# Transformed token blocks for the feed-forward products, built from PSUM and rounded earlier, with four additions fewer

## The reference, cut to what matters

```python
def conv_ffn(u, w_up, conv_w, conv_b, w_down):     # u: 512 x 1024, w_up: 1024 x 5632
    h = u @ w_up
    h = lax.conv_general_dilated(h, conv_w[:, None, :], window_strides=(1,),
                                 padding=((CONV_W - 1, 0),),
                                 dimension_numbers=('NWC', 'WIO', 'NWC'),
                                 feature_group_count=2 * D_FF) + conv_b
    gate, up = jnp.split(h, 2, axis=-1)
    return (jax.nn.gelu(gate, approximate=True) * up) @ w_down

# in reference():
        u = rmsnorm(h, g_pre_ffn[i])
        h = h + rmsnorm(conv_ffn(u, w_ffn_up[i], conv_w[i], conv_b[i], w_ffn_down[i]), g_post_ffn[i])
```

## Time and profile before

| | us |
|---|---|
| median of three runs | 853.69 |
| lowest and highest of them | 853.60, 855.11 |
| the profiled execution | 852.13 |
| its span, first to last instruction | 850.3 |
| TensorE busy | 835.8 (98%) |
| DVE busy | 652.0 (77%) |
| ACT busy | 477.4 (56%) |
| POOL busy | 399.8 (47%) |

### The profile page before, as it was taken

The page is one execution under the profiler, slowest core; times in us unless marked ns, Lnnn a source line. Parts: engine busy times, 40 slices in busy tenths (PEclk is TensorE's granted clock), DMA queues, the critical chain, the costliest instruction groups (busy, mean ns, idle before and its releaser), DMA issues.

```text
span 850.3 us, 13362 instructions
## 1 busy us (share of the span) xinstructions
PE 835.8 (98%) x4685; PEld 729.3 (86%) x4685; DVE 652.0 (77%) x1251; ACT 477.4 (56%) x898; POOL 399.8 (47%) x512
## 2 busy tenths in 40 slices
PE   8999999999999999999999999989999999999997
PEld 7888888888888888999998898879999999888885
DVE  6677787788766668965543589988888887799895
ACT  6566666877666654534452437365555554455562
POOL 5454434243333446986776427665555556100002
PEclk9999999999999999999999999999999999999999
DMA  7541233322223222343337432455544333745494
GB/s 218 164 126 51 71 80 95 94 78 80 82 81 81 63 62 65 110 137 100 88 123 255 142 125 85 157 167 167 167 120 118 118 118 119 278 162 195 151 290 156
DMA packets 138790, 109.24 MB, mean 128 GB/s; under 512 B 7559, under 2 KB 122191, under 8 KB 137700
## 3 DMA queue, kind: packets, MB, share of 16 engines
q1 hardware_dynamic: 137242, 101.00, 39.2%
q0 software_dynamic: 576, 4.19, 1.3%
q10 hardware_dynamic: 906, 3.20, 1.0%
HBM read 96.00 MB, written 12.37 MB: 127 GB/s over the span
## 4 chain that ended last, share of the span: by engine, by line
PE 87%; DVE 7%; DMA 2%; ACT 1%; POOL 1%; issue 1%; SPq 0%; DVEq 0%; ACTq 0%
PE banks L2234 22%; PE banks L2236 22%; PE banks L2235 22%; PE banks L2509 3%; PE banks L2511 3%; PE banks L2510 3%; PE banks L2410 2%; PE banks L2319 2%; PE banks L2318 2%; DVE wide L2060 2%; PE banks L2682 1%; PE banks L2681 1%; PE banks L2680 1%; PE banks L2382 1%; DMA ring_raw<-in_w_ffn_up_dram 1%; DVE pages L2001 1%
## 5 line engine op out<-in xcount | busy, mean ns | idle before, releaser
L845 POOL TENSOR_TENSOR ring_lo<-ring_raw,ring_hi 128x256 fp32r<-128x256 f32 x380 | 312.4, 854 | 271.5 <-ACT ring_hi L1001 271.2
L2234 PE MATMUL banks<-u_hi,ring_hi 128*128 128x512 f32 (+1 forms) x624 | 237.1, 380 | 2.5 <-DVE wide L2060 1.8
L2236 PE MATMUL banks<-u_hi,ring_lo 128*128 128x512 f32 (+1 forms) x624 | 232.2, 372 | 0.0
L2235 PE MATMUL banks<-u_lo,ring_hi 128*128 128x512 f32 (+1 forms) x624 | 232.0, 372 | 0.0
L2234 PEld LDWEIGHTS banks<-u_hi,ring_hi 128*128 128x128 f32 x624 | 118.1, 189 | 21.7 <-DVE wide L2060 2.0
L2236 PEld LDWEIGHTS banks<-u_hi,ring_lo 128*128 128x128 f32 x624 | 118.0, 189 | 20.9
L2235 PEld LDWEIGHTS banks<-u_lo,ring_hi 128*128 128x128 f32 x624 | 118.1, 189 | 18.6
L1001 ACT CAST ring_hi<-ring_raw 128x1024 fp32r<-128x1024 f32 x96 | 100.0, 1043 | 37.7 <-PE banks L2236 24.3
L2060 DVE SCALAR_TENSOR_TENSOR wide<-banks,cols,wide 128x511 f32<-128x511 f32 x88 | 64.8, 746 | 18.9 <-ACT wide L1361 11.4
L852 POOL TENSOR_SCALAR norm_ms<-norm_ss 128x1 f32<-128x1 f32 x15 | 6.0, 401 | 137.4 <-ACT pages L1011 137.3
L2234 PE MATMUL banks<-pages,ring_hi 128*128 128x512 f32 (+1 forms) x176 | 60.1, 341 | 0.0
(11 more groups left out here) (318 smaller groups left out, 1954.6 us busy)
## 6 DMA issues: line engine op xcount, KB each, us to landing
ring_raw<-in_w_ffn_up_dram SPq DMA_DIRECT2D x88, 256.0 KB, 3.4
ring_raw<-in_w_in_dram SPq DMA_DIRECT2D x60, 256.0 KB, 3.4
ring_raw<-in_w_ffn_down_dram SPq DMA_DIRECT2D x55, 256.0 KB, 3.4
ring_raw<-in_w_gate_dram SPq DMA_DIRECT2D x48, 256.0 KB, 3.2
ring_raw<-in_w_out_dram SPq DMA_DIRECT2D x16, 256.0 KB, 3.1
split_tokens<-pages SPq DMA_DIRECT2D x4, 1024.0 KB, 6.8
pages<-split_tokens POOLq DMA_DIRECT2D x4, 1024.0 KB, 11.9
second_tokens<-wide SPq DMA_DIRECT2D x10, 384.0 KB, 4.1
```

The costliest lines, as they stand in the source:

```text
L845: last = pool.tensor_tensor(wlo[:, r, c], raw[:, r, c], whi[:, r, c].bitcast(F32), ALU.subtract)
L2234: pe.matmul(out, lhs_hi, rhs_hi, start=start, stop=False)
L2235: pe.matmul(out, lhs_hi, rhs_lo, start=False, stop=False)
L2236: return pe.matmul(out, lhs_lo, rhs_hi, start=False, stop=stop)
```

## The change

`t_forms_12` makes T1 and T2 with the second token half read straight from banks 4 to 7 (`turned_half`) instead of from the sum of its high and low parts. So the additions of U12 and U22 fall away, two for each part, four in all. `t_forms_34` makes T3 and T4, with T3 now taken from T2 and U11 (T2 - U11). The order is changed on three engines. On DVE, T1 and T2 of part 1 come before the first taps, T3 and T4 of part 1 in their old place, and the low parts of all forms move from pair 1 into pair 0. On ACT, the forms are rounded one by one as each is made, ahead of the taps of unit 0 and of unit 1; in pair 1 the rounding of the weight forms of pair 2 moves ahead of `split_tokens(1)`. On TensorE, the wait for the low parts of the forms moves ahead of the first of the seven products. No matmul, no transfer and no instruction of POOL or SP is added or removed.

```diff
+        T_RAW = {1: 1, 2: 3, 3: 0, 4: 2}
+
+        def turned_half(row, c):
+
+            banks = psum[:, 4:8, :].rearrange("p (t h) (k n) -> p h k t n", h=2, n=P)
+            return banks[:, row, 2 * c:2 * c + 2, :, :]
...
-            def t_forms_high(c):
-
-                act.wait_ge(t_form_sums, 6 * c + 10)
-                for q in range(1, 5):
-                    act.copy(t_form(q, slice(2 * c, 2 * c + 2))[0], u_raw(U_RAW[q], c)).then_inc(t_form_hi, 1)
-
-            for j in range(2):
-                ffn_unit(j, None, j)
-                t_forms_high(j)
+            def t_forms_high(c, which=(1, 2, 3, 4)):
+
+                for q in which:
+                    act.wait_ge(t_form_sums, 4 + 4 * c + q)
+                    act.copy(t_form(q, slice(2 * c, 2 * c + 2))[0], u_raw(T_RAW[q], c)).then_inc(t_form_hi, 1)
+
+            t_forms_high(0)
+            ffn_unit(0, None, 0)
+            t_forms_high(1)
+            ffn_unit(1, None, 1)
...
             gelu(1, 1)
+            up_forms_high(2)
             split_tokens(1)
-            up_forms_high(2)
...
-            def t_sums_rest(c):
...
+            def t_forms_12(c):
+
+                t1, t2, r11 = (u_raw(q, c).rearrange("p k (t n) -> p k t n", n=P) for q in (1, 3, 0))
+                dve.tensor_tensor(t1, turned_half(0, c), r11, sub).then_inc(t_form_sums, 1)
+                dve.wait_ge(t_form_sums, 5 + 4 * c)
+                dve.tensor_tensor(t2, turned_half(1, c), t1, sub).then_inc(t_form_sums, 1)
+
+            def t_forms_34(c):
+
+                r11, r21, t2 = (u_raw(q, c) for q in (0, 2, 3))
+                dve.wait_ge(t_form_sums, 6 + 4 * c)
+                dve.tensor_tensor(r11, t2, r11, sub).then_inc(t_form_sums, 1)
+                dve.tensor_tensor(r21, r21, t2, sub).then_inc(t_form_sums, 1)
...
-            dve.wait_ge(u_lo_done, 2 * TT)
-            t_sums_rest(0)
+            dve.wait_ge(t_form_sums, 4)
+            t_forms_12(0)
+            t_forms_34(0)
+            t_forms_12(1)
...
             ffn_taps(0, None, 0, (0,))
-            t_sums_rest(1)
+            t_forms_34(1)
             ffn_taps(0, None, 0, (1,))
+            t_forms_low(0)
             ffn_product(0, 0, first_tokens)
             ffn_taps(1, None, 1)
+            t_forms_low(1)
             ffn_product(1, 1, second_raw[:, 0:512])
             token_sums(0)
...
                 ffn_taps(2 * i, i, 0, (0,))
-                if i == 1:
-                    t_forms_low(0)
-                else:
+                if i in SEVEN_UP:
                     up_forms_low(i)
                 ffn_taps(2 * i, i, 0, (1,))
                 ffn_product(2 * i, 0, first_tokens)
-                if i == 1:
-                    t_forms_low(1)
...
                 n = i - SEVEN_UP[0]
+                if n == 0:
+                    pe.wait_ge(t_form_lo, 8)
```

More of the change, by code:

```diff
@@ L2000, in t_forms_low @@
                     hi, lo = t_form(q, slice(2 * c, 2 * c + 2))
-                    dve.tensor_tensor(lo, u_raw(U_RAW[q], c), hi.bitcast(F32), sub).then_inc(t_form_lo, 1)
+                    dve.tensor_tensor(lo, u_raw(T_RAW[q], c), hi.bitcast(F32), sub).then_inc(t_form_lo, 1)
             def up_weight_sums(i):
@@ L2629, in seven_up @@
                 n = i - SEVEN_UP[0]
+                if n == 0:
+                    pe.wait_ge(t_form_lo, 8)
                 pe.wait_ge(w_lo_done, up_tile(i, 0) + 1)
                 one_of_seven(W_BANK, up_quarter(0, 0), quarter(0, 0)).then_inc(up_prod, 1)
-                if n == 0:
-                    pe.wait_ge(t_form_lo, 8)
-                else:
+                if n >= 1:
                     pe.wait_ge(up_edge, 2 * n)
```

## The result

The changed kernel takes 845.24 us (four executions, 845.11 to 845.29), the kernel before 853.64 in the same measurement (853.38 to 855.11): a ratio of 0.9898, with a 95% interval of 0.9881 to 0.9915. That is 8.4 us less.

A forecast was written before the change was run, and what follows sets the result against it. TensorE, busy 98% of the span, was taken as the bound, recoverable only at two waits for DVE and a slow-clock stretch. DVE's terms summed to -5.21 us at L2033, giving 848.5 us from the 853.69 median, range 846.6 to 850.9.

The forecast's parts named there:

- the first stop and its half clock: TensorE's 1.79 us idle before unit 2 near 521 and the 1.2 GHz stretch after it (1.73 us): both would go.
- the swap on ScalarE: `up_forms_high(2)` ahead of `split_tokens(1)`: removes DVE's idle before the first taps of unit 4, -1.97 us.
- I predict the median: Final step: 5.2 us off the profiled 852.13 gives 846.9; from the 853.69 median it predicts 848.5 us.
- the second stop: TensorE's 3.11 us wait for `up_edge` (L2033) before pair 2's last product, ending at 569.38; forecast to shrink to 1.4 us.
- rival 3: The clock falls behind the remaining stop, costing 1.73 us: saves 3.5, 850.2 us; chance 0.11.
- my cap of 6.6 us: Most that could be gained on TensorE: 1.79 idle, 1.73 slow clock and 3.11 idle, 6.63 us in all.
- two sums for six behind the first taps: DVE after unit 0's first tap pair makes two sums of half 1 instead of six: -4.31 us.
- The last row keeps its distance: DVE's order from the taps at 556.06 to L2033 is unchanged, so L2033 moves 5.2 us, from 568.81 to 563.6.
- Rival 1: ScalarE's idle is not used, so DVE's 1.97 us before 556.06 stay: saves 3.2, 850.5 us; chance 0.14.
- Rival 2: TensorE's second wait goes wholly, by 1.4 us more from DVE: saves 6.6, 847.1 us; chance 0.11.
- rival 4: The slow stretch at 523.8 has another cause and stays, losing only 0.3 us: 848.8 us; chance 0.10.
- Rivals 5 and 6: No change, L2033 held by something unmoved, 853.7 us (0.05 and 0.03 chances); or slower, late weight tile 8 starving TensorE.

The follow-up runs named there:

- b_again: The kernel before, unchanged, run and profiled again: median 853.91 us of twelve executions, the profiled one 852.46 us.
- b_fill1: The kernel before with 14 idle-time matmuls into an unused bank ahead of TensorE's first long wait: 853.59 us, ratio 1.0.
- b_fill2: The kernel before with 24 idle-time matmuls at TensorE's second long wait alone: 852.34 us, ratio 0.9985.

## Why the prediction was wrong

The mechanism held: the first stop and its half clock went, L2033's place on DVE decided, the wait that was left stood where I had put it (though with 0.47 us for a forecast of 1.4, and so not the longest), the swap on ScalarE took out 1.97 us to the hundredth, and the new idle in unit 2 was 1.37 us (forecast 1.41). None of the new waits of the rivals came. Wrong was the size, by 3.3 us, in two steps.

**First, the baseline (about 1.5 us).** The failed step is "I predict the median": I took the gain from one execution and subtracted it from the median of others, as if both had lost the same. The median stood 1.56 us above the profiled time, and I gave no reason for that. The runs show the reason: half clock behind the second stop, absent in the one profile and present in two of the four later ones in which that stop was not filled (b_again and b_fill1 have none), where it cost 2.55 and 1.57 us; with that stop filled (b_fill2) the median falls by 1.4 us. In rival 3 I took "3.11 us at the second place was not [followed by it]" as evidence that such a stop leaves the clock alone. It was one draw. The gain had one more term, some 1.4 us of clock behind the second stop, and my cap of 6.6 us left it out. What else parts the executions of before, which differ by up to 3 us at the same mean clock, stays open.

**Second, the sum for L2033 (5.2 forecast, 6.81 measured).** Up to the taps of unit 4 DVE moved by 556.06 - 550.23 = 5.83 us; the rest, 0.98 us, is from there to L2033. By my own terms, each measured from the start of its first instruction to the start of the next thing, in us:

| term | forecast | measured |
|---|---|---|
| two sums for six behind the first taps | -4.31 | -4.60 |
| the start, and the sums before those taps | 0 | -0.18 |
| `t_forms_low(0)` | 0 | +0.38 |
| `t_forms_low(1)` | +0.61 | +1.34 |
| products of units 0, 1, 2, 3 | 0 | -1.04 |
| token sums of pair 0 | -0.95 | -0.97 |
| weight sums of pair 2 | 0 | +0.21 |
| idle in unit 2, idle before unit 4 | +1.41 - 1.97 | +1.37 - 1.97 |
| taps, and what lies between instructions | 0 | -0.37 |
| from the taps of unit 4 to L2033 | 0 | -0.98 |

The step that failed is "The last row keeps its distance", and with it the zeros of the table: instructions which I did not move I counted at their old length. They lie at another time against POOL now, and their length hangs on that: the products of units 0 to 2 fell from 1.15, 0.93 and 1.25 to 0.68 and 0.69 (that of unit 3 rose from 0.69 to 0.93), and three of the four weight sums of pair 3 took 0.82, 0.69 and 0.68 us where before they had taken 0.94, 1.12 and 1.21, in a pause of POOL. In the other direction the low forms took 4.62 and 4.58: the second four lie beside POOL nearly as a whole, where I had taken the middle between beside it and not. I had used this effect for the instructions that I moved and for the token sums, and not for the others.

**The rivals.** Rival 1 is refuted by the 1.97 us that went. Rival 2, the whole second wait gone, was the nearest in the trace (2.6 of its 3.1 us). Rival 3 named the right danger, but it was before that had it. For rival 4, the first half clock did belong to the stop as far as the runs tell: it was gone in the two profiles in which TensorE was kept busy there. The section on HAM oscillation in "TensorE: Matmul & The Clock Gate" of the Trainium skill, which I cited there, blames longer gaps; here the trace has half clock behind 1.79 us in all four profiles of before, though not in that of b_fill2, which has the same first stop. My remark in rival 4, that a slow stretch ahead of L2033 would cost only 0.3 us, is what b_fill1 then showed from the other side. For the PSUM source, the 62 cycles that the Trainium skill gives in "VectorE: DVE Perf Modes" (section on the TRN2 errata) do not appear: 0.68 us against 0.69. Rivals 5 and 6 did not come: tile 8's low part began at 534.73, TensorE had no wait for it.

## What to carry to other kernels

When the median of plain executions lies above the profiled one, something costs time that this profile does not show: take further profiles, and compare them stretch by stretch, before subtracting from the median. The mean clock of an execution was too coarse for it here. Where an idle stop of TensorE goes, count the clock behind it too, but only if no later wait for the same engine gives it back. Where one engine's work slows another's, an edit that shifts a stretch in time changes the length of instructions that it doesn't touch, and these have to be priced at their new neighbours.

## What the runs showed of the hardware

- The same stop, at the same place and of the same length (3.10 or 3.11 us), was followed by none, 3.4 or 6.8 us of half clock (1.2 GHz) in three executions of one program; the two stretches cost 1.57 and 2.55 us.
- With the stop of 1.79 us filled by 14 matmuls that compute nothing, two profiles have the clock at 1.00 behind it; unfilled, four of five have half clock there. In the longer stop, 24 such matmuls took the median down by 1.4 us and the spread of the executions from 3.3 us to 1.1 us.
- DVE instructions with both inputs in SBUF, 128x512 in float32, took 0.68 to 0.69 us alone and up to 1.23, mostly 1.11 and more, beside POOL's subtractions; without three quarters of POOL's pieces in pairs 1 to 3 the whole program was 8.7 us faster.
